# Fetching the first pages, head and query rows of a stick-breaking stage during the phase ahead of it

## The reference

```
br_p = stick_breaking(q_p, k_p, v_p, pos_p, pos_p, sb_bias[j])            # 1024 prompt tokens, causal
k_past = cache_sb_k[j][page_table].reshape(Bd, past, SB_HEADS, HEAD_DIM)   # 8 samples x 16 pages x 128 tokens
v_past = cache_sb_v[j][page_table].reshape(Bd, past, SB_HEADS, HEAD_DIM)
br_s = stick_breaking(q_s, concat(k_past, k_s), concat(v_past, v_s), pos_s, kpos_s, sb_bias[j])
y = concat([branch * silu(gate), mo * silu(mgate)]) @ w_out                # mo: attention to the memory

# sb_block: z = q k^T * HEAD_DIM**-0.5 + bias; mask = kpos < qpos
log_beta = log_sigmoid(z)
log_rem  = where(mask, log_beta - z, 0)
later    = cumsum from the right (log_rem) - log_rem
out      = where(mask, exp(log_beta + later), 0) @ v
```

## Time and profile before

| | |
|---|---|
| median of 3 runs | 2793.11 us |
| profiled execution, its own time | 2799.44 us |
| its span in the profile | 2797.7 us |
| PE busy | 2451.6 us (88%) |
| PE weight loads | 2016.4 us (72%) |
| DVE busy | 1105.5 us (40%) |
| ACT busy | 799.7 us (29%) |
| POOL busy | 189.8 us (7%) |
| HBM read and written | 361.75 and 62.37 MB, mean 152 GB/s |

### The profile page before, as it was taken

The page is one execution under the profiler, slowest core; times in us unless marked ns, Lnnn a source line. Parts: engine busy times, 40 slices in busy tenths (PEclk is TensorE's granted clock), DMA queues, the critical chain, the costliest instruction groups (busy, mean ns, idle before and its releaser), DMA issues. The chain is left out here.

```text
span 2797.7 us, 42542 instructions
## 1 busy us (share of the span) xinstructions
PE 2451.6 (88%) x17157; PEld 2016.4 (72%) x17157; DVE 1105.5 (40%) x1804; ACT 799.7 (29%) x1518; POOL 189.8 (7%) x379
## 2 busy tenths in 40 slices
PE   5599999986599699999999997568999999995899
PEld 4599998975488599999999896444555455542787
DVE  5323144013311310111011103267888888875311
ACT  4311111122200322112210013234555555554200
POOL 0000000201000000000001111111101111110000
PEclk8799999988799799999999997678999999998999
DMA  5412210210533332333231202368999999974432
GB/s 173 150 51 79 78 48 25 84 68 30 207 110 91 107 107 92 108 110 113 92 123 54 84 24 72 104 215 310 346 345 373 337 372 342 355 249 147 160 91 70
DMA packets 202813, 426.34 MB, mean 152 GB/s; under 512 B 22965, under 2 KB 115233, under 8 KB 202601
## 3 DMA queue, kind: packets, MB, share of 16 engines
q1 hardware_dynamic: 192025, 386.53, 39.7%
q0 software_dynamic: 10592, 37.10, 3.5%
HBM read 361.75 MB, written 62.37 MB: 152 GB/s over the span
## 5 line engine op out<-in xcount | busy, mean ns | idle before, releaser
L80 PE MATMUL o_bank<-o_w_hi,o_y_hi 128*128 128x512 f32 x576 | 230.2, 400 | 59.8 <-DVE o_w_lo L1244 59.8
L1866 DVE STREAM_TRANSPOSE b_kt<-b_kraw 128x768 f32<-128x768 f32 x256 | 248.1, 970 | 16.9 <-DMA b_kraw<-in_cache_sb_k_dram 16.9
L81 PE MATMUL o_bank<-o_w_lo,o_y_hi 128*128 128x512 f32 x576 | 228.6, 397 | 0.0
L82 PE MATMUL o_bank<-o_w_hi,o_y_lo 128*128 128x512 f32 x576 | 228.0, 396 | 0.0
L80 PEld LDWEIGHTS o_bank<-o_w_hi,o_y_hi 128*128 128x128 f32 x576 | 110.8, 192 | 86.5 <-issue 45.7
L2025 PEld LDWEIGHTS b_krow<-b_kt,b_qd 128*32 128x32 f32 x3072 | 109.1, 115 | 85.8 <-issue 62.5
L2025 PE MATMUL b_krow<-b_kt,b_qd 128*32 128x128 f32 x3072 | 147.1, 288 | 12.7 <-DVE b_kt L1866 12.7
L1368 ACT ACTIVATE i_stage<-i_bank 128x352 f32<-128x352 f32 x108 | 50.1, 464 | 344.6 <-PE i_bank L82 344.6
L1978 PE MATMUL b_zbank<-b_qh,b_kh 128*128 128x512 f32 (+3 forms) x288 | 136.2, 558 | 14.1 <-DMA b_qh<-scratch_qT 14.1
L1737 ACT ACTIVATE b_spl_hi<-b_spl 128x512 fp32r<-128x512 f32 (+2 forms) x144 | 75.3, 523 | 236.8 <-DVE b_spl L1813 188.7
L80 PE MATMUL i_bank<-h_hT_hi,h_w_hi 128*128 128x352 f32 x432 | 141.0, 326 | 2.1 <-PEq L75 2.1
(11 more groups left out here) (306 smaller groups left out, 5539.3 us busy)
## 6 DMA issues: line engine op xcount, KB each, us to landing
b_kraw<-in_cache_sb_k_dram SPq DMA_DIRECT2D x256, 384.0 KB, 5.5
b_vpage<-in_cache_sb_v_dram SPq DMA_DIRECT2D x128, 768.0 KB, 6.5
o_y<-scratch_yT SPq DMA_DIRECT2D x18, 1024.0 KB, 6.6
o_w<-in_w_out_dram SPq DMA_DIRECT2D x16, 1024.0 KB, 5.2
h_w<-in_w_in_sb_dram SPq DMA_DIRECT2D x8, 1536.0 KB
i_w<-in_w_in_sb_dram SPq DMA_DIRECT2D x8, 1536.0 KB
h_w<-in_cache_mem_k_dram SPq DMA_DIRECT2D x16, 512.0 KB, 4.7
a_sq<-in_cache_mem_v_dram SPq DMA_DIRECT2D x16, 512.0 KB, 5.2
```

The costliest lines, as they stand in the source:

```text
L80: pe.matmul(out, stat_hi, mov_hi, start=first, stop=False)
L81: pe.matmul(out, stat_hi, mov_lo, start=False, stop=False)
L82: return pe.matmul(out, stat_lo, mov_hi, start=False, stop=last)
L1866: dve.transpose(kt[u % 2][:, :, :, x * Q:(x + 1) * Q].rearrange("p h f j -> p (h f) j"), kraw[u % NK][:, x, :].rearrange("p (f j) -> p f j ...
```

## The change

The stage's first loads move from its own start to the middle of the memory attention of layer 1.

- `Kit` gets a side, and the transposed rows are allocated on the right side of SBUF. `hctx.close()` releases them (with their three semaphores) between the two blocks of the memory attention, in both layers. In layer 1 the class `StickAhead` then allocates in their place `kraw0`, `kraw1`, `vpage0` to `vpage4`, `qs`, the page table, and the head tiles `qh`, `kh`, `vh`, `gh`. `kraw2` is a view of `w`, which stays allocated until the stick-breaking stage ends; there its kit (13 semaphores) is released.
- SP calls `following.fetch(sp)` in the second block of the memory attention, between the memory value loads 3 and 4, after a wait for the last turned memory key.
- Head 0's values and gate are now loaded there by SP, not by GpSimd; also value pages 0 to 2.
- On SP the waits stand ahead of `value_load`; value pages 3 and 4 are loaded in unit 4 (was 8).
- On DVE the four transposes of unit 0 stand first. `unit(u, 0)` on PE waits for its own half of `qd` only.

```diff
@@ memory_attention_phase
                         ins.then_inc(s["ready"], 1)
+        hctx.close()
+        following.allocate()
         st = k.sb("st", [P, 4, NC])
...
                 sp.wait_ge(s["mean"], 1)
                 for b in range(NB_S):
+                    if b == BL:
+                        sp.wait_ge(s["ktr"], 2 * NB_S)
+                        following.fetch(sp)
                     if b >= BL:
                         sp.wait_ge(s["spv"], b // BL)
                     sp.dma_start(mv[:, b % BL, :, :], A["cache_mem_v"][i, b]...
@@ class StickAhead
+    def fetch(self, sp):
+        A, O, S = self.A, self.O, self.S
+        sp.dma_start(self.pages[:, :], A["page_table"]...).then_inc(self.paged, 16)
+        sp.dma_start(self.kh[:, 0, :], S["kT"][0, :, 0:SEQ]).then_inc(self.scored, 16)
+        sp.dma_start(self.qh[:, 0, :], S["qT"][0, :, 0:SEQ]).then_inc(self.scored, 16)
+        for x in range(PG):
+            sp.dma_start(self.qs[x * (P // PG):(x + 1) * (P // PG), :, :], S["qT"]...).then_inc(self.queried, 16)
+        sp.wait_ge(self.paged, 16)
+        self.keys(sp, 0)
+        sp.dma_start(self.vh[:, 0, :, :], O["sbv_p"]...).then_inc(self.rest, 16)
+        sp.dma_start(self.gh[:, 0, :], S["gT"][0, :, 0:SEQ]).then_inc(self.rest, 16)
+        sp.dma_start(self.kn[:, :, :], S["kT"]...).then_inc(self.added, 16)
+        sp.dma_start(self.qn[:, :, :], S["qT"]...).then_inc(self.added, 16)
+        sp.dma_start(self.vn[:, :], O["sbv_s"]...).then_inc(self.added, 16)
+        for u in range(1, NK):
+            self.keys(sp, u)
+        for n in range(NV - 2):
+            self.values(sp, n)
@@ stick_phase, sync
+                sp.dma_start(gs[:, :, :], S["gT"][:, :, SEQ:T]...).then_inc(s["gsl"], 16)
                 for e in order:
                     if e[0] == "K" and e[2] == 0:
                         if e[1] + NK < NU:
-                            keys(e[1] + NK)
-                        if 4 <= e[1] < 4 + NV - 2:
-                            values(e[1] - 4)
-                        if e[1] == 8:
-                            values(NV - 2)
-                            values(NV - 1)
+                            sp.wait_ge(s["ktr"], PG * (e[1] + 1))
+                            begun.keys(sp, e[1] + NK)
+                        if e[1] == 4:
+                            sp.wait_ge(s["nz"], 3)
+                            begun.values(sp, NV - 2)
+                            begun.values(sp, NV - 1)
@@ stick_phase, gpsimd
                 queries(0)
-                head(0)
-                head_gate(0)
@@ stick_phase, vector
+                for x in range(PG):
+                    turn(0, x)
                 negated(0)
                 negated(1)
                 softplus(0)
...
                 ins.then_inc(s["biased"], 1)
-                for x in range(PG):
-                    turn(0, x)
                 for e in order:
@@ stick_phase, tensor, unit
-                        pe.wait_ge(s["qb"], 2 * PG * (i + 1))
+                        pe.wait_ge(s["qb"], 2 * PG * i + PG * (half + 1))
```

More of the change, by code:

```diff
@@ L1456, in stick_phase, with allocate, fetch @@
+class NothingAhead:
+    def allocate(self):
+        pass
+    def fetch(self, sp):
+        pass
+def stick_phase(nc, c, A, O, S, begun):
     Q = P // PG
@@ L1561, in stick_phase @@
         new = lambda t, r=P: t[0:r, 0:NC_].rearrange("p (h t) -> p h t", h=HEADS)
-        kn, qn = (new(vpage[NV - 1][:, n * NC_:(n + 1) * NC_]) for n in range(2))
+        kn, qn = begun.kn, begun.qn
         zn, xn = (new(vpage[NV - 1][:, n * NC_:(n + 1) * NC_], SAMPLES) for n in range(2, 4))
         an = new(dz[:, 1, :], SAMPLES)
-        vn = vpage[NV - 2][0:SAMPLES, :]
+        vn = begun.vn
         view = lambda t, b: t[:, b % 2, :].rearrange("p (g h x t) -> p g h x t", g=2, h=HEADS, x=PG)
@@ L1570, in _ @@
             def _(sp):
-                def keys(u):
-                    g, half = group(u)
-                    for x in range(PG):
[L1574 to L1588, removed]
-                    sp.dma_start(vpage[n % NV][:, :], A["cache_sb_v"][0, bass.ds(page, 1)].rearrange(
-                        "o s h d -> (o s) (h d)")).then_inc(vl[n % NV], 16)
@@ L1603, in _ @@
-                for u in range(1, NK):
-                    keys(u)
+                sp.dma_start(gs[:, :, :], S["gT"][:, :, SEQ:T].rearrange("h p t -> p h t")).then_inc(s["gsl"], 16)
                 for e in order:
@@ L2082, in new_tokens @@
                     if m == 0:
-                        pe.wait_ge(s["nl"], 32)
+                        pe.wait_ge(begun.added, 48)
                         for h in range(HEADS):
@@ L2171, in program @@
-            if i:
-                stick_phase(nc, c, A, O, S)
+            with ExitStack() as lctx:
+                c["w"] = Kit(nc, lctx, f"l{i}_", "right").sb("w", [P, KD, KU])
+                with ExitStack() as hctx:
+                    kh = Kit(nc, hctx, f"h{i}_", "right")
+                    hT_hi = kh.sb("hT_hi", [P, KD, T], F32R)
+                    hT_lo = kh.sb("hT_lo", [P, KD, T], F32R)
+                    c["w_hi"], c["w_lo"] = (kh.sb(n, [P, KD, KU], F32R) for n in ("w_hi", "w_lo"))
+                    c["ahead_loaded"], c["ahead_hi"], c["ahead_lo"] = (
+                        kh.sem(n) for n in ("ahead_loaded", "ahead_hi", "ahead_lo"))
+                    if i == 0:
+                        front_phase(nc, c, A, O, S, hT_hi, hT_lo, x_rows)
+                        pool_phase(nc, c, A, O, {"yT": S["yT0"]}, hT_hi, hT_lo)
+                        w_in, q0, following = A["w_in_pool"][0], 2 * BW, NothingAhead()
+                    else:
+                        norm_phase(nc, c, A, hT_hi, hT_lo, x1_rows, i)
+                        in_phase(nc, c, A, O, S, hT_hi, hT_lo)
+                        w_in, q0, following = A["w_in_sb"][0], 4 * BW, StickAhead(nc, lctx, c, A, O, S)
+                    with ExitStack() as mctx:
+                        km = Kit(nc, mctx, f"mem{i}_")
+                        c["mkT"], c["mv"] = km.sb("mkT", [P, MH, MEM]), km.sb("mv", [P, MJ, MW])
+                        memory_attention_phase(nc, c, A, O, S, S[f"yT{i}"], i, w_in, q0, q0 + MW, hT_hi, hT_lo, hctx,
+                                               following)
+                if i:
+                    stick_phase(nc, c, A, O, S, following)
```

140 lines of the change are left out of this document (71 added, 69 removed).

## The result

The changed kernel takes 2780.19 us (median of 7 runs, 2778.45 to 2783.76) against 2797.47 us before (7 runs, 2790.53 to 2805.52): ratio 0.9942, 95% interval 0.9931 to 0.9953. That is 16.2 us less (13 to 19), where 29.4 us less was forecast. The profiled execution took 2778.97 us. It is faster, as forecast, but by little more than half as much: 2780.19 lies above the range of 2755 to 2774.

A forecast was written before the change was run, and what follows sets the result against it. It saw PE busy 88% of the span, but the stick-breaking stage short of data at its start and near unit 8. 23.6 - 0.4 + 5.2 + 1.5 - 0.5 = 29.4 us off 2793.1 gave 2763.7, range 2755 to 2774.

The forecast's parts named there:

- The start: Start of the stick-breaking stage: with data in place, unit 1's first transpose comes 23.6 us earlier, less 0.4 us loss on PE.
- The value page: Stick-breaking stage near unit 8: loading pages 3 and 4 in unit 4 removes PE's wait for page 3, gain 5.2 us.
- The clock around that page: Stretch around the late value page: without the stall the granted clock stays higher, gain 1.5 us, ends 0 and 3.0.
- The estimated 5 us: Same clock term by the Trainium skill's formula, throttled time x (1 - 1.2/2.4); the prediction took 1.5 us instead.
- The clock elsewhere: Start of the stick-breaking stage: the clock may rise a step earlier or later, 4 us either way, taken as 0.
- The fetch in the memory attention: Second block of layer 1's memory attention: the 27 loads fit before SP's next duty, cost 0, upper end 2 us.
- The meetings: Meetings of all engines: one moved to mid-phase in both layers, one added behind the stick-breaking stage, 0.5 us loss (0.3 to 1.2).
- SP's later order: SP in the stick-breaking stage: the wait ahead of the register load delays each unit's keys, hidden by 12 us of room, cost 0.
- PE's readiness at the start: Start of the stick-breaking stage: PE ready at about 1814.9, DVE releasing it at about 1814.3; loss taken as 0.4 us.
- The memory attention pays: Rival: the fetch takes twice as long and delays the second half of the memory values by 18 us, 2782; chance 0.05.
- the second memory attention between the same two marks within 1 us: Sign in the changed profile: the second memory attention keeps its length within 1 us; growth above 2 us would refute the forecast.

The follow-up runs named there:

- right_only: The kernel before with only the weight tile w, transposed rows, w_hi and w_lo allocated on the right side of SBUF: ratio 1.0031 to before.
- fetch_late: The changed kernel with the whole fetch issued at the start of the stick-breaking stage instead of in the memory attention: ratio 1.0027 to before.
- pages_late: The changed kernel with value pages 3 and 4 loaded in unit 8 as before: ratio 0.9957 to before.
- right_release: As right_only, plus the transposed rows released between the two blocks of the memory attention, nothing fetched ahead: ratio 1.0042 to before.
- after_again: The changed kernel, unchanged, run once more: ratio 0.9944 to before.
- before_again: The kernel before, unchanged, run once more: ratio 1.0008 to before.
- only_memory_right: The changed kernel with everything on the left of SBUF except the memory attention's tiles, which go right: 2773.47 us, ratio 0.9916 to before.

## Why the prediction was wrong

What failed is a step that the prediction did not have. It took the allocation of the rows and weights on the other side of SBUF as free: "Sum. 23.6 - 0.4 + 5.2 + 1.5 - 0.5" has no term for it, and it gives no reason for leaving it out. right_only prices it at 8.7 us (3 to 14). It is paid in the pool and the input projection, two phases that the prediction never looked at.

Point by point, in its own steps:

- The start, 23.6 less 0.4: 22.8 us measured at units 2 to 4, 22.3 in the second pair of profiles. Right within 1 us. fetch_late confirms that the data's being there is the cause.
- The value page, 5.2: between units 9 and 10 the lead grows from 24.2 to 29.5 us; pages_late gives 5.5. Right.
- The clock around that page, 1.5 (0 to 3): at most 1 us, 0.3 in the unit of the wait and up to 0.7 in the two behind it. The term was too large by 0.5 us or more: the clock does fall there, but the stretch is hardly longer than the wait makes it. The estimated 5 us beside it were further off still.
- The clock elsewhere, 0 (4 either way): between units 4 and 5 the lead grew by 1.6 us in one pair of profiles and fell by 2.9 in the other. The ends were fair; which way it goes changes from one execution to the next.
- The fetch in the memory attention, 0: right, 129.2 against 129.1 us. The fetch has 6 loads with runs of 128 bytes, not 7; nothing hangs on it.
- The meetings, 0.5: by the profile the two in the middle take 0.4 and 0.6 us, the one behind the stage 0.6, and 0.4 is saved twice: 0.8, within its ends. right_release leaves room for 3 us in the timed runs.
- SP's later order, 0: right. No wait of DVE for keys is left in the changed kernel.
- PE's readiness at the start, "about 1814.9": its own terms, 1809.9 + 1.9 + 1.5 + 2.0, give 1815.3, and the loss 1.0 and not 0.4; still within its ends.

The profiles show where the rest of the difference lies. Mean of changed and after_again against mean of before and before_again, each rounded:

| phases | us |
|---|---|
| stick-breaking stage (29.9 forecast) | -29.0 |
| pool and input projection | +8.3 |
| the two memory attentions | +2.9 |
| the release behind the stage | +0.6 |
| all others | -0.7 |
| whole span | -18.0 |

So the part that the prediction worked out came as forecast, and the places took 8.3 us of it back. The 2.9 us of the memory attentions can't be told from their spread: the two profiles of the kernel before differ by 3.7 us there. The stage's 29.0 is a mean of 27.2 and 30.7, so its closeness to 29.9 is in part luck. only_memory_right shows the same from the other side: without the loss of the places the gain is 23.5 us (20 to 27), 7 more than the changed kernel's, but still short of 29.4 by 2 to 9 us. That remainder isn't assigned by any run.

4.4 of the 16.5 us between 2763.7 and 2780.19 come from the starting point: the prediction subtracts from 2793.11, the median of three runs, and the seven have 2797.47.

None of the rivals was this one. "The memory attention pays" gives 2782, near the measured time, but by a wait that didn't occur; the agreement is chance. The test written down, "the second memory attention between the same two marks within 1 us", wouldn't have found the loss either: that phase is 1.2 us longer than in the first profile of before, no more than it varies by itself. The length of each untouched phase did.

## What to carry to other kernels

Compare the length of every phase, the untouched ones first: a change that reuses memory also moves tiles, and here that had a price (8 us) which no instruction list shows. Where an early release forces something to the other side, keep the two operands of the long matmul phases together, and move the short phase: that gave 7 us back here. Before fetching data under another phase, work out two times, bytes over the rate and issues times their spacing, and see that both end before the queue's next duty; here they ended 9 us before it, and the fetch cost nothing that could be seen. Change the order of the engine that uses the data only together with the fetch.

## What the runs showed of the hardware

Two phases of the same matmuls at the same granted clock took up to 1.4% longer by the place of the tiles: the pool 360.4 to 365.6 us, the input projection 592.4 to 600.2 us. The products whose rows and weights lie on opposite sides of SBUF are the longer ones, 423.5 against 419.4 to 420.5 us over 1296 matmuls in the largest case. One placement repeats within 1 us (the changed kernel's over seven profiles: 363.4 to 364.3 and 597.5 to 598.1).

A fall of the granted clock can cost nothing or several us. A wait of 5.1 to 6.6 us for a page, with the clock of its stretch at 0.69 to 0.78, cost the wait and at most 1 us more; other falls in the same stage cost 0.8 to 4.4 us. One program's stage differs by 3 to 7 us between two executions (739.2 and 742.4, 766.4 and 773.1 us), and apart from the unit of the late page the units that differ are those with such a fall.
